# Norm hand-offs by halves of the tokens, and the last norm applied in token rows, in a two-block layer kernel

## The reference, cut to what matters

```
x = x + rms_norm(attention(rms_norm(x, mix_pre0)), mix_post0)      # stages gate, pair, sig, ao
x = x + rms_norm(conv_ffn(rms_norm(x, ffn_pre0)),  ffn_post0)      # stages up2, down2
x = x + rms_norm(delta_net(rms_norm(x, mix_pre1)), mix_post1)      # stages rate, qkv, og, do
x = x + rms_norm(conv_ffn(rms_norm(x, ffn_pre1)),  ffn_post1)      # stages up3, down3
out = x without the 16 meta tokens
rms_norm(y, w) = y * rsqrt(mean over 1024 features of y*y + eps) * w
```

## Time and profile before

| | us |
|---|---|
| median of 3 runs (range) | 2637.31 (2634.67 to 2639.53) |
| the profiled execution, its time | 2638.41 |
| its span | 2636.5 |

### The profile page before, as it was taken

The page is one execution under the profiler, slowest core; times in us unless marked ns, Lnnn a source line. Parts: engine busy times, 40 slices in busy tenths (PEclk is TensorE's granted clock), DMA queues, the critical chain, the costliest instruction groups (busy, mean ns, idle before and its releaser), DMA issues.

```text
span 2636.5 us, 44461 instructions
## 1 busy us (share of the span) xinstructions
PE 2489.4 (94%) x19232; PEld 2204.0 (84%) x19232; DVE 1351.1 (51%) x2057; ACT 974.4 (37%) x1558; POOL 961.6 (36%) x553
## 2 busy tenths in 40 slices
...
DMA packets 379858, 201.26 MB, mean 76 GB/s; under 512 B 6400, under 2 KB 377088, under 8 KB 379664
## 3 DMA queue, kind: packets, MB, share of 16 engines
...
## 4 chain that ended last, share of the span: by engine, by line
PE 61%; DVE 12%; ACT 5%; issue 2%; POOL 1%; POOLq 0%; ACTq 0%; DVEq 0%
PE ps L677 48%; DVE t_ffy L2945 3%; DVE t_atq L2739 2%; ACT t_wh L645 1%; PE ps L2547 1%; PE ps L3180 1%; PE ps L2520 1%; DVE t_ffy L2948 1%; PE ps L2486 1%; PE ps L3199 1%; ACT t_ffy L2848 1%; PE ps L3203 1%; DVE t_ainv L2767 1%; DVE t_wl L655 1%; PE ps L519 1%
## 5 line engine op out<-in xcount | busy, mean ns | idle before, releaser
L655 POOL TENSOR_TENSOR t_wl<-t_raw,t_wh 128x1024 fp32r<-128x1024 f32 (+2 forms) x196 | 443.5, 2264 | 804.3 <-ACT t_wh L645 804.3
L677 PE MATMUL ps<-t_hh,t_wh 128*128 128x264 f32 (+2 forms) x1712 | 402.9, 314 | 12.1 <-DVE t_dcq L2673 3.6
L645 ACT ACTIVATE t_wh<-t_raw 128x1024 fp32r<-128x1024 f32 (+2 forms) x253 | 255.5, 1012 | 416.8 <-PE ps L677 372.1
L677 PE MATMUL ps<-t_hh,t_wl 128*128 128x264 f32 (+2 forms) x1712 | 379.2, 300 | 6.3 <-POOL t_wl L655 3.1
L677 PE MATMUL ps<-t_hl,t_wh 128*128 128x264 f32 (+2 forms) x1712 | 376.1, 301 | 0.0
L677 PEld LDWEIGHTS ps<-t_hh,t_wh 128*128 128x128 f32 x1712 | 269.9, 191 | 37.0 <-issue 19.8
L677 PEld LDWEIGHTS ps<-t_hh,t_wl 128*128 128x128 f32 x1712 | 269.5, 190 | 22.9 <-issue 6.3
L677 PEld LDWEIGHTS ps<-t_hl,t_wh 128*128 128x128 f32 x1712 | 269.1, 191 | 14.6 <-issue 7.1
L2945 DVE SCALAR_TENSOR_TENSOR t_ffy<-t_ffp,t_vec,t_ffy 128x528 f32<-128x528 f32 (+1 forms) x88 | 176.5, 2005 | 178.9 <-ACT t_ffy L2848 178.9
L655 POOL TENSOR_TENSOR t_fwl<-t_raw,t_fwh 128x1024 fp32r<-128x1024 f32 (+1 forms) x72 | 168.0, 2335 | 153.3 <-ACT t_fwh L645 153.3
L677 PE MATMUL ps<-t_fhh,t_wl 128*128 128x512 f32 (+1 forms) x704 | 211.6, 341 | 2.9 <-POOL t_wl L655 2.8
(11 more groups left out here) (571 smaller groups left out, 5429.4 us busy)
## 6 DMA issues: line engine op xcount, KB each, us to landing
...
```

The lines of the kernel that those rows point to most:

```text
L645: ac.activation(wh[slot_of[j]][:, 0:kc, :], raw[r % NRAW][:, 0:kc, :], ACT.Copy).then_inc(up("wh_cut", "cut", j), 1)
L655: eng.tensor_tensor(wl[slot_of[j]][:, 0:kc, :], raw[r % NRAW][:, 0:kc, :], wh[slot_of[j]][:, 0:kc, :].bitcast(F), SUB).then_inc(up(name, " ...
L677: ins = pe.matmul(ps[bank_of(j, i)][:, 0:tn], wt[slot][:, k, :], a[:, k, t0:t0 + tn], start=first, stop=last)
```

## The change

1. The last four panels in front of q=1, 2 and 3, and the last three in front of q=4, are made in halves of the tokens: first the first half of all of them, then the second half of all of them (`half_panel`). Sums, roots and spread of the first half stand among the second halves. The first few x of the first half too (`EARLY_X`). The next stage's three panels are fed half by half (`fed_by_sides`), the third panel two chunks behind the others. The filler matmuls of q=1 to 3 are gone. Take, square and add of these panels go by halves, the adds on DVE instead of POOL.
2. The low weight cuts of the first panels of up2, rate, qkv and up3 go from POOL to DVE. do1 uses two more weight slots.
3. `gst_zero` goes from in front of q=2's x to behind the products of the stage's first panel.
4. `finish(1)` is queued in front of do0, and waits longer between its sums and its products (14 steps instead of 5). do1's first two panels are made chunk by chunk together (`weave`).
5. At q=4 x goes to token rows early: 32 transposes of x stand among down3's products (`xturn`). Behind the last panels, y is turned by matmuls with a diagonal matrix of the post weights (`rturn`, 32 of 128x128), and one DVE instruction per 128 tokens and 512 features multiplies by the reciprocal root, which is then a scalar of each partition, and adds x (`final`, 8 of them). There is no spread and no x on POOL. Each of the 8 results is stored by a DMA when it is there.
6. Roots and reciprocals are taken in equal slices by one instruction each (528 tokens as 6 of 88) instead of two.

```diff
+        SIDES = {1: HALF, 2: HALF, 3: [(0, 272), (272, 256)], 4: [(NM, 256), (NM + 256, 256)]}
+        ENDS = {1: ("ao", 0, 4), 2: ("down2", 2, 4), 3: ("do", 1, 4), 4: ("down3", 2, 3)}
+        HALVED = {}
+        for q, (stage, group, n) in ENDS.items():
+            for j in range(end_of(stage, group) - n, end_of(stage, group)):
+                HALVED[j] = q
+                panels[j] = panels[j]._replace(spans=SIDES[q])
...
-        THIRD = [first_of("gate") + 2, first_of("rate") + 2]
-        WIDE = [("ao", "up2", "down2"), ("up3", "down3")]
+        THIRD = [first_of("gate") + 2, first_of("rate")]
+        WIDE = [("ao", "up2", "down2"), ("do1", "up3", "down3")]
...
-            if p.stage in ("rate", "qkv") and j in FED:
-                low_on[j] = "wl_pool"
+            elif j == THIRD[1]:
+                slot_free[j] = end_of("up2", 2) - 1
+            if j in FED:
+                low_on[j] = "wl_pool" if p.stage in ("gate", "pair") else "wl_dve"
...
+                elif panels[j].stage == "do":
+                    w.wait_ge(s.lo_dve, at("lo_dve", "fmul", 1, 2))
+                    w.wait_ge(s.lo_pool, at("lo_pool", "fmul", 1, 3))
...
+        def fed_by_sides(js, a):
+            for i in range(2):
+                for c in range(KD + 2):
+                    if c < KD:
+                        if i or c >= early_x[a]:
+                            put_x(a, c, i)
+                            put_high(a, c, i)
+                        for j in js[:2]:
+                            put("mm", j, c, 0, i)
+                            put("mm", j, c, 2, i)
+                    if c >= 2:
+                        put("mm", js[2], c - 2, 0, i)
+                        put("mm", js[2], c - 2, 2, i)
...
+        def half_panel(q, j, i, at_mid=None):
+            for k in range(panels[j].kc):
+                for m in range(3):
+                    put("mm", j, k, m, i)
+                if at_mid and k == panels[j].kc // 2 - 1:
+                    at_mid()
+            sig.mark(*(("mm_done", j, 0) if i == 0 else ("mm_done", j)))
+            put("take_h", j, i)
+            sig.mark(half_by(j, i), "take", j, i)
+            put_square_h(q, panels[j].m, i)
...
+        def end_by_sides(q):
...
+            for j in js:
+                half_panel(q, j, 0)
+                cut_freed(js[0] - 1, j)
+            roots_of_sides(q)
+            for x, j in enumerate(js):
+                half_panel(q, j, 1, (lambda: put_spread(POST[q][0], side_banks[q][0:1])) if x == 1 else None)
+                if x == 0:
+                    put_roots(POST[q][0], side_banks[q][0:1])
+                cut_freed(j, j)
+                for _ in range(EARLY_X[q][x - 1] if 0 < x < 3 else 0):
+                    put_x(q, early_x[q], 0)
+                    put_high(q, early_x[q], 0)
+                    early_x[q] += 1
...
+        def end_in_rows():
...
+            half_panel(4, js[0], 0)
+            put("rturn", 0, 0, use=spare[0:1])
+            half_panel(4, js[1], 0)
+            put("rturn", 1, 0, use=spare[1:2])
+            half_panel(4, js[2], 0)
+            roots_of_sides(4)
+            half_panel(4, js[0], 1)
+            put_roots(POST[4][0], [bank_of(js[0], 0)])
+            put("rturn", 0, 4, use=[bank_of(js[1], 0)])
+            put("rturn", 1, 4, use=[bank_of(js[2], 0)])
+            put("final", 0, 0)
+            put("final", 1, 0)
+            half_panel(4, js[1], 1)
+            put("final", 0, 4)
+            put("rturn", 2, 0, use=spare[0:1])
+            put("rturn", 3, 0, use=spare[1:2])
+            half_panel(4, js[2], 1)
+            put("final", 1, 4)
+            put("rturn", 2, 4, use=[bank_of(js[0], 1)])
+            put("rturn", 3, 4, use=[bank_of(js[1], 1)])
+            put_roots(POST[4][1], [bank_of(js[0], 0)])
+            for i in (2, 3):
+                for c0 in (0, 4):
+                    put("final", i, c0)
...
                     gemm((up_,), then_early, group=g + 1, pair=True)
-                gemm((down,), post_sums(q, down, 2) if g == 2 else None, tail=g == 2, group=g, two=True)
-            flush()
-            post_root(q)
+                if n and g == 0:
+                    put("diag")
+                gemm((down,), post_sums(q) if g == 2 else None, group=g, two=True, mid=turn_x_beside if n else None)
+            (end_in_rows if n else lambda: end_by_sides(q))()
             ready_at[up_] = lambda p, k: [("lo_dve", "low", a, k)]
             ready_at[down] = lambda p, k: [("lo_pool", "uconv1", n, GROUPS[p.group][0] + k)]
...
+                put("gst_zero")
...
-            for _ in range(5):
+            for _ in range(14 if G else 5):
...
-        put("gst_zero")
...
+        behind.append(finish(1))
         gemm(("do",), None, every=4, group=0)
-        behind.append(finish(1))
         drain()
         sqb_last[:] = [("scaled", "fsum", 1), ("conved", "dtap", 7, 2)]
-        gemm(("do",), post_sums(3, "do", 1), tail=True, group=1)
-        flush()
-        post_root(3)
+        gemm(("do",), post_sums(3), group=1, weave=True)
+        end_by_sides(3)
...
-        SIGNALS["turn_out"] = "turned"
-        for c in range(KD):
-            put_x(4, c)
-        for c0 in range(0, KD, 4):
-            for i in range(4):
-                put("turn_out", c0, i, banks=1, of=8)
-                sig.mark("scaled" if c0 and i % 2 else "copied", "turn_out", c0, i)
 
...
+            def rturn(i, c0):
+                b, = bank("rturn", i, c0)
+                held(b)
+                w.wait_ge(s.copied, at("copied", "diag"))
+                for c in range(c0, c0 + 4):
+                    j = first_of("down3", 2) + c
+                    e = ("took_d", "take", j, i // 2) if j in HALVED else ("took_d", "take", j)
+                    w.wait_ge(handles[e[0]], at(*e))
+                    ins = pe.matmul(ps[b][:, 128 * (c - c0):128 * (c - c0) + 128],
+                                    acc[1][c][:, NM + 128 * i:NM + 128 * i + 128], diag[0][:, c, :], start=True, stop=True)
+                ins.then_inc(up("turned", "rturn", i, c0), 1)
+                free[b] = [(s.scaled, at("scaled", "final", i, c0))]
...
+                dv.scalar_tensor_tensor(out=o, in0=ps[bank("rturn", i, c0)[0]][:, :],
+                                        scalar=roots[POST[4][i // 2] % 4][:, i % 2:i % 2 + 1], in1=o, op0=MUL,
+                                        op1=ADD).then_inc(up("scaled", "final", i, c0), 1)
```

More of the change, by code:

```diff
@@ L262, in program @@
         for j, p in enumerate(panels):
-            wide = next((4 + 2 * i for i, stages in enumerate(WIDE) if p.stage in stages), None)
+            wide = wide_of(p)
             if wide is None and len(turns) == 4:
@@ L427, in gemm @@
                 begin = 3
+            elif sides:
+                cut_to(js[2], js[0])
+                kept.update(bank_of(j, i) for j in js[:3] if slot_of[j] == 3 for i in range(2))
+                fed_by_sides(js, sides)
+                cut_to(js[3], js[0])
+                for j in js[:3]:
+                    taken(j, then, keep=keep)
+                kept.clear()
+                begin = 3
             if two:
```

485 lines of the change are left out of this document (305 added, 180 removed).

## The result

| | before | changed |
|---|---|---|
| median of 12 runs (range), us | 2638.87 (2634.32 to 2643.32) | 2647.22 (2643.14 to 2649.02) |
| span of the profiled execution, us | 2636.5 | 2643.0 |

The ratio is 1.0028, with an interval of 1.0020 to 1.0036: the changed kernel is slower, by 8.35 us in the medians, where 19 us faster were forecast and 2634 was the upper end of the range.

A forecast was written before the change was run, and what follows sets the result against it. PE, busy 94% of the span, was taken as the bound. End -11.9, gated norm -8.0, q=1 -1.3, q=2 -0.3, q=3 +0.8, clock +1.7 sum to -19.0: from 2638.4 to 2619 us, range 2609 to 2634.

The forecast's parts named there:

- What bounds the kernel: Whole kernel: PE is busy 94% of the span, so gains come only where PE waits, runs slowly, or behind its last product.
- The end's added work: q=4, in front of the last product: 56 transposes and turning matmuls at 0.107 us, sums, narrower products; 6.7 us added.
- The gated norm: State's output to do1: squares start 10.7 us sooner, beside do0's last four panels; 8 us won.
- The hand-offs: q=1 to 3: feeding by halves wins 1.3 us at q=1 and 0.3 at q=2, loses 0.8 at q=3.
- The sum for q=1: From ao's last product to the next stage's fourth panel: products, small matmuls, waits and last copy, 30.6 us instead of 31.9.
- the clock: Lower granted clock behind PE's waits: 1.7 us lost at q=3, nothing at the other hand-offs.
- that rival sum: By the skill's half-rate rule, q=1 and q=2 lose 1.7 us each too: 3.4 more, total 2622.8.
- The first (hand-offs give back, 2630 to 2641): Rival, chance 0.15: DVE's waits at q=1 to 3 twice as long as walked, 11 to 22 us worse.
- The second: Rival, chance 0.08: clock stays down through all three hand-offs, 2640.7 us, or 2645 with the gated norm's gain halved.
- The third: Rival, chance 0.09: advancing the gated norm doesn't pay, as do0's panels wait for cuts behind it; 2627 us.
- the fourth: Rival, chance 0.10: all waits come out short, DVE running ahead under half panels; 6 to 9 us more won, about 2612.

## Why the prediction was wrong

**What bounds the kernel** was read rightly: the end and the gated norm are where the time was, and both won. Behind the last product 7.9 was forecast and 8.0 came, with a `final` of 0.68 to 0.75.

**The end's added work** was put at 6.7 and is 9.6 (3.5 + 6.1): the price of a transpose was taken for a matmul of the same shape. 24 turning matmuls in front of the last product at 0.224 instead of 0.107 are 2.8 more, and the run with transposes gave 2.7 back. The Trainium skill, "FP8 and Floating Point Precision", section TensorE Precision Notes, states that a true FP32 product takes four passes through the array; no run here shows the passes, only two records of such a matmul where a transpose has one, and 2.1 times the transpose's time. So the end won 8.2 to 8.9 and not 11.9.

**The gated norm** was right in place, but too large by some 2 to 3 us: 5.7 up to do1's second panel, 5.2 over do with whole hand-offs, for 8.0. The waits walked came no longer than walked (1.72 for 1.7, 4.29 for nearly 6). Not in the walk were the 2.08 among the norm's own products; how much of the rest is the clock, 0.62 there, no run separates. Beside the halves only part of the gain is seen in the changed kernel's do (-2.8), since do1's last four panels take 20.5 us there for 17.5 before.

**The hand-offs are the step that failed.** The forecast was -1.3, -0.3 and +0.8, with 1.7 for the clock. Against the kernel before, the three stretches came out at +4.0, +9.4 and +1.6, with 2.9 more in do1's last panels; against whole hand-offs the halves cost 21.2. The waits were sized well: 6.05 with the last copy's 0.62 for 7.5 + 0.6 at q=1, 5.88 for 5.7 at q=2's end, 4.85 for 5.6 at q=3. What failed is PE's own work at full clock and the clock.

The first is the larger. The sum for q=1 had 17.7 for the products and 4.8 for the small matmuls, 22.5 to the fourth panel. With fillers, at full clock, they take 20.2 and 5.8 from start to start, waits and fillers apart. The kernel before takes 18.1 and 6.9 by the same count, 25.0: the sum was 2.5 short even of the kernel that it was compared with, and that is more than the 1.3 won. The small matmuls were priced like transposes here too, and by halves the products take 2.1 more. The sums and spread of the first half, moved in front of ao's last product, were put at nothing; that group is 1.1 longer at q=1, and 1.4 at q=2. And the forecast counted the sooner start of PE as a gain, although the fillers it replaced kept nothing waiting: the last x comes 2 to 4 us later than before, since the second half's x can't start before a spread that is queued behind the first half's products, and 16 half x's take longer than 8 whole ones, as forecast. In all, q=1's fourth panel starts 34.9 us behind ao's last product (33.2 with fillers) for 30.6 forecast.

The second is the clock: 1.7 at q=3 and nothing elsewhere. Up to the 144th fed product the run with fillers took back 1.7 at q=1, 4.4 at q=2 and 0.5 at q=3, 6.6 in all. The prediction had the measure at hand: a 3.59 us wait with a clock of 0.69 behind it. It used that for the longest wait alone, and took q=1's first wait, put at 3.6, for free. By the rule of the Trainium skill, "TensorE: Matmul & The Clock Gate", Part 1, that half rate is the default and work lifts it, q=1 and q=2 were to pay as well; the trace agrees (0.51 behind 2.91 us, 0.67 at q=2). At 1.7 each that rival sum was right at q=1, too small at q=2, where the clock is under 1.00 in all three windows, and too large at q=3. A slow stretch also delays the second half's sums and spread, which stand in the same queue, and so lengthens the next wait.

**The rivals.** The first (hand-offs give back, 2630 to 2641) had the right place, but not the reason: the waits were not twice as long, and with DVE's cuts on POOL the time is the same. The second had the right side, with a chance of 0.08, and the cause of a third to a half of the loss. The third fell with the 5.2 to 7.4 that the advance won, the fourth with waits that came out about as walked. The range was too narrow since three hand-offs were bounded one by one and share one cause.

**Open**: how the part that came back with the fillers divides between the halves and the wait at q=2's end, and why a wait of the same length slows the clock in one run and not in another. With only q=3 by halves do is 2 us longer than in the changed kernel (106.0 and 104.0 in one trace each); most of it is the clock in the second halves of do1's last panels, 0.83 from 2202.4 to 2212.5 there and 1.00 from 2217.4 to 2225.9 in the changed kernel, with a wait of 1.24 and 1.22 us in it.
